# First block of a two-block model: value units first, decay chain inside the attention heads, and a new order at the latent attention's entrance

## The chip, the cores and the metric

One core of a Trainium2 chip (trn2). The metric is the device time of one execution in microseconds (us); smaller is better. Everything runs in one launch.

## The reference

The first block is a hybrid layer on 512 tokens of width 1024. What the change touches:

```python
h = rms_norm(x, mix_norm)
z = h @ w_in                       # 19 column tiles of 128
gq, gk, gv, gr, glr, sq, sk, sv = split_cols(z, SPLITS)
log_a = log_sigmoid(glr @ w_alpha2 + b_alpha) / 16
o_gla = gla_chunked(gq * 64 ** -0.5, gk, gv, log_a)   # 4 heads, chunks of 64
o_gla = rms_norm(o_gla, gla_norm) * silu(gr)
o_swa = swa_sink_attention(rms_norm(sq, q_norm), rms_norm(sk, k_norm), sv, sinks)
                                   # 8 heads, window 128, ALiBi
x = x + concat([o_gla, o_swa]) @ w_out
...                                # convolved, gated feed-forward
```

In `gla_chunked`, b is the running sum of log_a in a chunk; q exp(b) meets k exp(-b) under a causal mask, k exp(b_last - b) makes a state for each chunk, and the states are carried on with the factor exp(b_last). The second block (two layers) has a latent attention, of which the change touches the entrance:

```python
c_kv = rms_norm_2(hn @ w_dkv, kv_norm_g)      # rank 256
k_rope = apply_rope(hn @ w_kr, cos, sin)
k_nope, v = c_kv @ w_uk, c_kv @ w_uv          # 8 heads of 128
q = rms_norm_2(hn @ w_dq, q_norm_g) @ w_uq    # rank 384, 8 heads of 128 + 64
s = (q_nope k_nope^T + q_rope k_rope^T) * 192 ** -0.5, masked, softmax, @ v
```

## The kernel before

**Data.** Activations lie transposed (features on the 128 partitions, 512 tokens along the row), eight tiles for width 1024. Every weight matrix is cut into units of 128 x 1024 numbers, 283 in all (512 KB each), which SyncE loads in order into a ring of four buffers `w_raw`. Float32 accuracy comes from three passes: ScalarE copies a unit to `w_hi` (fp32r), VectorE writes the rest to `w_lo`, and likewise `a_hi`, `a_lo` for activations; `three` multiplies hi by hi, hi by lo and lo by hi. A unit is 24 matmuls of 512 columns. Plain float32 matmuls are used for scores, transposes, sums and spreads.

**Order.** Each engine runs one program written out by hand, and only semaphores tie them together: `unit_ready` (TensorE waits for w_lo), `unit_done` (VectorE waits for the last matmul of a unit), `out_read` (a bank of PSUM has been read), `k_ready` (an operand's low part is there). `w_hi_of(n)` on ScalarE and `lo_ahead(n)` on VectorE prepare the unit three ahead; each waits until its ring slot is free. Waits stand in the queue, so that everything behind one of them waits too.

**The input product** ("z", 19 units): 4 tiles of sliding-window queries (z_sq), keys, values, 4 tiles of linear-attention q and k, the low-rank gate, 4 gate tiles (z_r), and last four units for the linear attention's values, which are computed with tokens on the partitions (`z_v`). At the start `three_tiles` interleaves three tiles over k as the rows of x land, while ScalarE squares each row and GpSimd adds the squares up (`add_squares`); `stat` sums over the partitions, a root and a reciprocal follow, and `spread` brings the factor to all partitions (`r_pre`). Then come tiles 3 and 4, the sums of squares of the five head tiles in a row (`token_sums`), tile 5, the key factors and the turned values.

**The eight window heads** are a pipeline over i from -1 to 7. In a step TensorE makes the scores of head i + 1 (L1244), one z tile, the values of head i - 1 (L1273) and the transposes of head i (L1259). VectorE prepares a w_lo, adds the bias and takes the maximum of head i + 1, normalises head i (L1794), reads the z tile (L1812) and evacuates the transposes. ScalarE prepares a w_hi (L613), takes the exps of head i + 1 (L700) and evacuates the other half (L719).

**The linear attention.** The gate's logits come in steps 4 and 5. Behind the heads, beside the value units, runs the decay chain on two engines: Abs, Exp, Ln (ScalarE), log gate (L1824), two scans (L1827), exps and products. Then scores (L1316), transposes, chunk states, masked products, carried states, and for each head sum of squares, root, factor, spread, gate and split, before the output product ("wout", 8 units, four banks), and "upA".

**The latent entrance** (from 1240 us): units dkv (3), dq (3), uk (2), uq (6), uv (2). A unit's tiles are read by VectorE after the whole unit, rotary embedding is done for each pair of heads after the q units, four products with constants (`run_idle`) stand in front of the first scores, and both value units are done before them.

## Time and profile before

| | |
|---|---|
| median of 3 runs | 1814.08 us (1810.33 to 1817.05) |
| the profiled execution | 1813.4 us, its span on the core 1811.6 us |
| TensorE busy | 1771.5 us (98%) |
| VectorE, ScalarE, GpSimd busy | 986.7, 620.4, 194.3 us |
| mean granted clock of TensorE | 0.992 |

Starts and stretches are in us from the first instruction of the span. Busy times count an engine's own instructions; a stretch in which TensorE is busy throughout can still run at the lower clock, which PEclk shows as a share of full speed.

### The profile page before, as it was taken

To read this page: it belongs to the slowest core of one execution; us is meant where nothing else is said; L and a number is where in the kernel's file an instruction comes from. 1 tells how busy PE (TensorE), PEld (TensorE's weight loads), DVE (VectorE), ACT (ScalarE), POOL (GpSimd) and SP (SyncE) were. 2 spreads that over 40 slices of the span, in tenths; PEclk is the share of its full clock that TensorE was granted. 3 is DMA by queue.
4 is the path that set the end of the run, shared out by engine and by line. 5 is a ranking of instruction groups with operands and counts; after the bars stand their busy time and mean duration, and the time that the engine had idled before them with its cause. 6 is when DMAs were issued, how large, how long until landed. Compare 5 with 4: busy or idle time off the path is not lost.

```text
span 1811.6 us, 21991 instructions
## 1 busy us (share of the span) xinstructions
PE 1771.5 (98%) x8104; PEld 1436.8 (79%) x8104; DVE 986.7 (54%) x1322; ACT 620.4 (34%) x909; POOL 194.3 (11%) x175
## 2 busy tenths in 40 slices
PE   6999999999999999999999999999999999999998
PEld 5777888888888888877888888877767788888886
DVE  4666446673565489985642344346675564234432
ACT  4345234442343342244422222234253433112221
POOL 2100021110011200101110011000000111001111
PEclk9999899999999999999999999999999999999999
DMA  5212023333233222312233233221310223223321
GB/s 181 88 47 70 13 92 113 94 106 115 84 102 100 75 93 93 105 59 94 79 96 104 93 93 102 95 82 58 92 37 1 94 82 104 93 93 95 103 82 46
DMA packets 43844, 156.05 MB, mean 86 GB/s; under 512 B 4864, under 2 KB 4992, under 8 KB 43776
## 3 DMA queue, kind: packets, MB, share of 16 engines
q1 hardware_dynamic: 43632, 154.19, 26.8%
q8 instruction: 46, 0.75, 0.2%
q10 hardware_dynamic: 144, 0.92, 0.1%
q14 instruction: 22, 0.18, 0.0%
HBM read 153.00 MB, written 2.10 MB: 86 GB/s over the span
## 4 chain that ended last, share of the span: by engine, by line
PE 94%; DVE 4%; ACT 1%; issue 1%; DMA 0%; SPq 0%; ACTq 0%; DVEq 0%
PE bank L1023 27%; PE bank L1024 27%; PE bank L1025 27%; PE bank L1168 1%; PE bank L1174 1%; PE bank L1169 1%; PE bank L1244 1%; DVE w_lo L1695 1%; PE bank L1064 1%; PE bank L1273 1%; PE bank L1110 1%; PE bank L1628 1%; PE bank L1098 0%; PE bank L1058 0%; PE bank L1259 0%
## 5 line engine op out<-in xcount | busy, mean ns | idle before, releaser
L1695 DVE TENSOR_TENSOR w_lo<-w_raw,w_hi 128x1024 fp32r<-128x1024 f32 x283 | 364.9, 1292 | 314.3 <-ACT w_hi L613 191.5
L1023 PE MATMUL bank<-a_hi,w_hi 128*128 128x512 f32 x1156 | 460.3, 398 | 20.1 <-DVE w_lo L1695 17.4
L1024 PE MATMUL bank<-a_lo,w_hi 128*128 128x512 f32 x1156 | 455.7, 394 | 0.0
L1025 PE MATMUL bank<-a_hi,w_lo 128*128 128x512 f32 x1156 | 453.5, 392 | 0.0
L1023 PEld LDWEIGHTS bank<-a_hi,w_hi 128*128 128x128 f32 x1156 | 218.7, 189 | 74.6 <-issue 15.1
L1023 PE MATMUL bank<-g_hi,w_hi 128*128 128x512 f32 x688 | 270.1, 393 | 0.0
L1024 PE MATMUL bank<-g_lo,w_hi 128*128 128x512 f32 x688 | 270.0, 392 | 0.0
L1025 PE MATMUL bank<-g_hi,w_lo 128*128 128x512 f32 x688 | 267.6, 389 | 0.0
L1025 PEld LDWEIGHTS bank<-a_hi,w_lo 128*128 128x128 f32 x1156 | 218.4, 189 | 49.1
L1024 PEld LDWEIGHTS bank<-a_lo,w_hi 128*128 128x128 f32 x1156 | 218.9, 189 | 46.2 <-issue 1.0
L613 ACT ACTIVATE w_hi<-w_raw 128x1024 fp32r<-128x1024 f32 x167 | 174.4, 1050 | 196.5 <-PE bank L1025 191.3
L623 ACT ACTIVATE w_hi<-w_raw 128x1024 fp32r<-128x1024 f32 x116 | 121.6, 1048 | 130.3 <-PE bank L1025 130.3
L1025 PEld LDWEIGHTS bank<-g_hi,w_lo 128*128 128x128 f32 x688 | 129.1, 188 | 29.2
L1023 PEld LDWEIGHTS bank<-g_hi,w_hi 128*128 128x128 f32 x688 | 129.2, 188 | 29.1
L1024 PEld LDWEIGHTS bank<-g_lo,w_hi 128*128 128x128 f32 x688 | 129.3, 188 | 26.5
L531 POOL TENSOR_TENSOR tmp<-tmp 128x512 f32<-128x512 f32 x64 | 66.6, 1041 | 490.4 <-DVE tmp L2120 490.4
L926 ACT ACTIVATE g_hi<-tmp 128x512 f32 (+1 forms) x64 | 40.4, 632 | 219.8 <-DVE tmp L2120 219.8
L510 POOL TENSOR_TENSOR ssum<-ssum,tmp 128x512 f32<-128x512 f32 x43 | 62.6, 1455 | 477.5 <-ACT tmp L636 476.3
L2124 DVE TENSOR_TENSOR g_lo<-tmp,g_hi 128x512 f32 (+1 forms) x64 | 44.3, 693 | 89.3 <-POOL tmp L531 89.3
L2010 DVE SCALAR_TENSOR_TENSOR cv<-u_pad,cols,cv 128x512 f32<-128x512 f32 x128 | 91.1, 780 | 0.0
L2120 DVE SCALAR_TENSOR_TENSOR tmp<-bank,r_pre 128x512 f32<-128x512 f32 x64 | 44.2, 690 | 81.1 <-PE bank L1025 76.0
L520 POOL TENSOR_TENSOR tmp<-tmp 128x512 f32<-128x512 f32 x22 | 34.6, 1573 | 283.4 <-ACT tmp L814 283.4
(288 smaller groups left out, 1987.4 us busy)
## 6 DMA issues: line engine op xcount, KB each, us to landing
w_raw<-in_stream SPq DMA_DIRECT2D x283, 512.0 KB, 3.5
h<-in_xT SPq DMA_DIRECT2D x8, 256.0 KB, 6.4
out<-h SPq DMA_DIRECT2D x8, 256.0 KB, 2.1
cst_b<-in_consts SPq DMA_DIRECT2D x1, 896.0 KB, 9.8
cst_b<-in_consts ACTq DMA_DIRECT2D x1, 896.0 KB, 4.5
cols<-in_vectors SPq DMA_DIRECT2D x1, 289.0 KB, 2.8
cst<-in_consts SPq DMA_DIRECT2D x1, 257.0 KB, 8.2
w_al<-in_w_alpha SPq DMA_DIRECT2D x1, 128.0 KB, 9.8
```

Source lines behind the costliest of these rows:

```text
L510: pool.tensor_tensor(ssum[:, :], ssum[:, :], sq_buf[(k - 1) % 2], ALU.add).then_inc(sum_added, 1)
L531: pool.tensor_tensor(tmp[2 + j % 2][:, 0:SEQ], tmp[j % 2][:, 0:SEQ], tmp[j % 2][:, 0:SEQ], ALU.mult).then_inc(hid_sq, 1)
L613: act.activation(w_hi[slot][:, :], w_raw[slot][:, :], ACT.Copy).then_inc(whi_ready, 1)
L623: act.activation(w_hi[slot][:, :], w_raw[slot][:, :], ACT.Copy).then_inc(whi_ready, 1)
L926: act.activation(at(g_hi, 4 * i + j), tmp[j % 2][:, 0:SEQ], ACT.Square)\
L1023: pe.matmul(out, w0, x0, start=start, stop=False, skip_group_check=loose)
L1024: pe.matmul(out, w0, x1, start=False, stop=False, skip_group_check=loose)
L1025: return pe.matmul(out, w1, x0, start=False, stop=stop, skip_group_check=loose)
L1695: dve.tensor_tensor(w_lo[slot][:, :], w_raw[slot][:, :], f(w_hi[slot][:, :]), ALU.subtract)\
L2010: dve.scalar_tensor_tensor(T(cv, c), u_pad[:, c * UW + tap:c * UW + tap + SEQ], col("w_dw", c * CONV_W + tap), T(cv, c), ALU.mult, ALU.add)\
L2120: dve.scalar_tensor_tensor(tmp[j % 2][:, 0:SEQ], bank[j][:, :], 0.0, r_pre[:, :], ALU.max, ALU.mult).then_inc(out_read, 1)
L2124: dve.tensor_tensor(at(g_lo, 4 * i + j), tmp[2 + j % 2][:, 0:SEQ], f(at(g_hi, 4 * i + j)), ALU.subtract).then_inc(x_ready, 1)
```

## The change

It reorders the z product and what hangs on it, and has seven parts.

1. The stream of units starts with the four value units (15 to 18), then keys, z_sq 0 and 1, values of the window heads, low-rank gate, z_sq 2 and 3, q and k, gate tiles. The value units run over x rows in the order in which they land, two rows to a unit. TensorE first multiplies zeros four times (512 columns, float32) as soon as GpSimd has cleared `ssum`. The eight columns of `mix_norm` are loaded ahead of x, the other vectors behind it, and ScalarE takes a root of a constant before x is there.
2. Squares of x go to `m` and are folded by VectorE instead of being summed by GpSimd; their sums over partitions come inside the last value unit.
3. The sums of squares of the head tiles come one at a time inside later tiles; their roots too.
4. The heads begin with eight units done. Logits come in steps 0 and 1, two of the sums of squares in step 2, and the decay chain is spread over steps 2 to 7 on both engines. Two gate tiles are in the heads' last steps.
5. The other two gate tiles are cut in two and stand between the linear attention's parts, as do halves of the first two output tiles. Output tiles go round eight banks. Roots and reciprocals are taken for two heads at once, all sums in one bank.
6. upA's first tiles wait only for the banks they write.
7. Latent entrance: uk and uv tiles are signalled one by one, bank rules name the exact read, w_hi of the first q unit goes ahead of r_post's copy, rope is done a unit earlier with its low parts behind, the products with constants are gone, the second value unit stands behind the first scores, and two output units are prepared in heads 1 and 2.

The diff, cut:

```diff
+Z_UNITS = [15, 16, 17, 18, 4, 0, 1, 5, 10, 2, 3, 6, 7, 8, 9, 11, 12, 13, 14]
...
-IN_M = ("ffpre0", "pre1", "ffpre1")
+IN_M = ("mix", "ffpre0", "pre1", "ffpre1")
...
 # SyncE
-            sp.dma_start(cols[:, :], vectors).then_inc(vec_landed, 16)
+            sp.dma_start(cols[:, 0:KD], vectors[:, 0:KD]).then_inc(vec_landed, 16)
...
+            sp.dma_start(cols[:, KD:], vectors[:, KD:]).then_inc(vec_landed, 16)
...
 # GpSimd
+            pool.memset(ssum[:, :], 0.0).then_inc(zeroed, 1)
             pool.memset(z_sk[:, 0:P], 0.0).then_inc(p_zero, 1)
-            add_squares("mix")
...
 # ScalarE
+            act.wait_ge(v_chain, 1)
+            load_sqrt(len(STATS))
...
-                square("mix", k, T(h, k))
-            w_hi_of(AHEAD, AHEAD)
+                square_in_m(k)
+            for n in range(RING, RING + 3):
+                w_hi_of(n, n % RING)
             act.wait_ge(v_chain, 2)
-            take_root("mix", r_pre)
+            take_root("mix", None)
+            w_hi_of(RING + 3, RING - 1)
+            spread_copy("mix", r_pre)
...
             for i in range(-1, SWA_H):
-                n = z0 + 6 + i + 1
+                n = z0 + 8 + i + 1
                 w_hi_of(n + AHEAD, (n + AHEAD) % RING)
...
+                if i == 3:
+                    act.wait_ge(a_chain, 1)
+                    act.activation(gla_e, gla_e, ACT.Exp, scale=-1.0).then_inc(a_chain, 1)
+                if i == 5:
+                    act.wait_ge(gla_cum, 2)
+                    act.activation(gla_e, gla_b, ACT.Exp, scale=1.0 / 16).then_inc(gla_exp, 1)
+                if i == 6:
+                    act.wait_ge(gla_ops, 1)
+                    act.activation(gla_e, gla_b, ACT.Exp, scale=-1.0 / 16).then_inc(gla_exp, 1)
+                if i == 7:
+                    act.wait_ge(gla_cum, 3)
+                    act.activation(gla_b, gla_b, ACT.Exp, scale=1.0 / 16).then_inc(gla_exp, 1)
                 if i + 1 < SWA_H:
                     swa_exp_of(i + 1)
+                if i == 3:
+                    act.wait_ge(a_chain, 2)
+                    act.activation(gla_e, gla_e, ACT.Ln, bias=1.0).then_inc(gla_l, 1)
...
                     act.activation(swa_pt[i % 2][:, SEQ:], bank[6][:, :], ACT.Copy).then_inc(swa_ea, 1)
+                if i == 0:
+                    gla_logit_of(0)
+                if i == 1:
+                    swa_square(3, T(z_sq, 2), 10)
+                    swa_square(4, T(z_sq, 3), 11)
+                    gla_logit_of(1)
+                if i == 2:
+                    swa_root(3, 2)
+                    act.wait_ge(gla_y, 2)
+                    act.activation(gla_e, gla_b, ACT.Abs).then_inc(a_chain, 1)
...
 # TensorE
-            three_tiles("z", a_hi, a_lo, "mix", "mix")
+            pe.wait_ge(zeroed, 1)
+            for _ in range(4):
+                pe.matmul(bank[7][:, :], ssum[:, 0:P], ssum[:, :], start=True, stop=True)
+            for u in range(4):
+                unit_ready(u)
+                for k in (2 * u, 2 * u + 1):
+                    k_ready("mix", k)
+                    for b in range(NB):
+                        last = three(bank[b][:, :], T(a_hi, k)[:, b * P:(b + 1) * P], T(a_lo, k)[:, b * P:(b + 1) * P],
+                                     T(w_hi[u], k % 2), T(w_lo[u], k % 2), k == 0, k == KD - 1)
+                    if k == 6:
+                        folded_stat("mix")
+                last.then_inc(unit_used, 1)
+            spread("mix")
...
+            gla_scores_of(0)
+            gla_scores_of(1)
+            pe.wait_ge(gla_ops, 3)
+            gla_turn(0)
+            swa_values(SWA_H - 1)
+            gla_turn(1)
+            z_tile(17, 6, 0, 4)
+            pe.wait_ge(gla_tr_read, 2)
+            gla_chunks(0)
+            gla_inner(0)
+            gla_inner(1)
+            z_tile(17, 6, 4)
...
+            gla_chunks(1)
+            gla_carried(0)
+            gla_inner(2)
+            gla_inner(3)
+            z_tile(18, 7, 0, 4)
+            gla_carried(1)
+            gla_mean_square(0)
+            gla_mean_square(1)
+            z_tile(18, 7, 4)
+            gla_factors(0)
+            gla_factors(1)
+            gla_mean_square(2)
+            gla_mean_square(3)
+            wout_part(0, True)
+            gla_factors(2)
+            gla_factors(3)
+            wout_part(1, True)
...
 # VectorE, in the heads' loop, after the z tile is read
+                if i == 2:
+                    swa_r_of(3, 2)
+                if i == 4:
+                    gla_log_gate()
+                    gla_cumulate(0)
+                if i == 5:
+                    gla_cumulate(1)
+                    dve.wait_ge(gla_cum, 2)
+                    dve.tensor_copy(b_last[:, :], chunks[:, :, CHUNK - 1]).then_inc(gla_blast, 1)
+                if i == 6:
+                    dve.wait_ge(gla_exp, 1)
+                    dve.scalar_tensor_tensor(z_q[:, :], z_q[:, :], GLA_DK ** -0.5, gla_e, ALU.mult, ALU.mult)\
+                        .then_inc(gla_ops, 1)
+                if i == 7:
+                    dve.wait_ge(gla_exp, 2)
+                    dve.tensor_tensor(chunks, last.broadcast_to([P, 2 * NCH, CHUNK]), chunks, ALU.subtract)\
+                        .then_inc(gla_cum, 1)
+                    dve.tensor_tensor(gla_e, gla_e, z_k[:, :], ALU.mult).then_inc(gla_ops, 1)
...
 # latent entrance: TensorE
-                last.then_inc(unit_used, 1)
+                    last.then_inc(uk_done if j < 3 else unit_used, 1)
...
-            pe.wait_ge(out_read, TILE0["uv"] + 1)
-            run_idle(0, 4)
-            pe.wait_ge(rope_split, 10)
...
+            uv_tiles(0)
+            pe.wait_ge(rope_split, 10)
             for b in range(NB):
                 mla_scores(0, b)
+            uv_tiles(1)
```

## Rows read from the trace of the kernel before

**Rows 1.** Stretches, core 0: their sum, with each engine's busy time.
```profile
sum 1811.60, PE 1771.55 PEld 1436.83 DVE 986.67 ACT 620.41 POOL 194.28; mean PE 161.05 PEld 130.62 DVE 89.70 ACT 56.40 POOL 17.66
```

**Rows 2.** Stretches: length, busy time (instructions) by engine, PEclk, DMA share, GB/s.
```profile
34.00:67.00 33.00, 30.97 (x167) 26.05 (x168) 11.92 (x16) 12.17 (x18) 3.04 (x2) 0.90 0.26 80
67.00:177.00 110.00, 109.98 (x543) 86.39 (x541) 73.83 (x146) 47.82 (x108) 8.94 (x6) 1.00 0.18 58
...
177.00:206.00 29.00, 24.81 (x257) 23.79 (x256) 16.43 (x37) 10.78 (x20) 1.84 (x2) 0.83 0.11 38
...
180.00:190.00 10.00, 8.63 (x131) 8.10 (x132) 7.12 (x18) 3.89 (x7) 0.00 (x0) 1.00 0.18 63
...
1254.00:1282.00 28.00, 23.59 (x113) 19.24 (x113) 15.37 (x23) 9.01 (x14) 1.28 (x1) 0.94 0.28 85
1282.00:1312.00 30.00, 28.39 (x117) 21.67 (x117) 20.26 (x28) 6.94 (x8) 0.00 (x0) 1.00 0.31 90
1312.00:1342.00 30.00, 26.58 (x121) 19.27 (x122) 24.49 (x45) 18.93 (x40) 0.00 (x0) 1.00 0.21 68
```

**Rows 3.** Waits of TensorE to 300 us: total us, times, longest us.
```profile
PE bank L1023 <- DVE w_lo L1695: 14.7, 3, 9.0
PE bank L1316 <- DVE z_v L1848: 2.8, 1, 2.8
...
PE bank L1023 <- DVE h L1894: 0.9, 1, 0.9
```

**Rows 4.** Timeline, TensorE, entrance: start, duration, engine, line, operation.
```profile
20.31 0.63 PE L1025 MATMUL bank<-a_hi,w_lo 128*128 128x512 f32 x1
20.73 0.63 PE L1023 MATMUL bank<-a_hi,w_hi 128*128 128x512 f32 x1
...
33.25 0.39 PE L1024 MATMUL bank<-a_lo,w_hi 128*128 128x512 f32 x1
33.48 0.39 PE L1025 MATMUL bank<-a_hi,w_lo 128*128 128x512 f32 x1
```

**Rows 5.** Timeline, TensorE: sums of squares (L1058) and head 0's scores (L1244).
```profile
54.63 1.86 PE L1058 MATMUL bank<-cst,tmp 128*128 128x2 f32 x8 [1.36 <-ACT tmp L683]
...
65.46 1.99 PE L1244 MATMUL bank<-z_sk,z_sq 64*128 64x256 f32 x8 [0.27 <-DVE z_sk L1760]
```

**Rows 6.** Timeline of one step of the heads, by engine.
```profile
102.14 1.99 PE L1244 MATMUL bank<-z_sk,z_sq 64*128 64x256 f32 x8
...
111.44 0.98 PE L1259 MATMUL bank<-cst,swa_p 128*128 128x128 f32 x7
...
102.74 1.05 ACT L613 ACTIVATE w_hi<-w_raw 128x1024 fp32r<-128x1024 f32 x1
...
103.82 1.23 DVE L1695 TENSOR_TENSOR w_lo<-w_raw,w_hi 128x1024 fp32r<-128x1024 f32 x1 [0.70 <-ACT w_hi L613]
...
109.88 0.69 DVE L1812 TENSOR_TENSOR z_lr<-bank,r_pre 128x512 f32<-128x512 f32 x1
```

**Rows 7.** Groups of ScalarE, 67 to 165 us: busy us, mean ns.
```profile
L700 ACT ACTIVATE swa_p<-swa_p,small 128x256 f32<-128x256 f32 x32 | 15.8, 494 | 0.0
...
L733 ACT ACT_TABLE_LOAD x1 | 1.3, 1283 | 0.0
```

**Rows 8.** Timeline, VectorE: log gate (L1824) and the two scans.
```profile
165.25 1.23 DVE L1824 SCALAR_TENSOR_TENSOR m<-m 128x1024 f32<-128x1024 f32 x1 [3.73 <-ACT m L733]
...
166.51 2.34 DVE L1827 TENSOR_TENSOR_SCAN m<-cst_b,m 128x512 f32<-128x512 f32 x2
```

**Rows 9.** Waits of TensorE, 1254 to 1345 us.
```profile
PE bank L1023 <- DVE w_lo L1695: 2.7, 1, 2.7
PE bank L1023 <- issue: 1.7, 1, 1.7
...
PE bank L1628 <- DVE q_rot L2200: 1.6, 1, 1.6
```

**Rows 10.** Timeline, TensorE: the products with constants.
```profile
1323.13 3.59 PE L1064 MATMUL bank<-cst 128*128 128x512 f32 x8
```

More of the change, by code:

```diff
@@ L477, in _ @@
             sp.dma_start(w_al[:, :], w_alpha).then_inc(cst_landed, 16)
+            z_rounds = len(Z_UNITS) // RING
+            for n in range(RING, RING + RING * z_rounds):
+                load(n, n % RING)
             def four(i):
@@ new lines, in gla_root_of, with gla_out_of @@
+            def gla_root_of(t):
+                c = RC_GLA + 2 * NB * t
+                act.wait_ge(gla_sums, 2 * t + 2)
+                act.activation(rms[:, c:c + 2 * NB], bank[6][:, 2 * NB * t:2 * NB * t + 2 * NB], ACT.Sqrt,
+                               bias=small[:, 60:61]).then_inc(gla_rms, 1)
+            def gla_out_of(hd):
+                act.wait_ge(o_done, hd + 1)
+                act.activation(T(og_hi, hd), tmp[hd][:, 0:SEQ], ACT.Copy).then_inc(xhi_ready, 1)
+            gla_square(0)
@@ L768, in _ @@
+            gla_square(1)
+            load_sqrt(len(STATS) + 1)
+            gla_root_of(0)
+            gla_square(2)
+            gla_square(3)
+            gla_root_of(1)
+            w_hi_of(UNIT0["wout"] + AHEAD, (UNIT0["wout"] + AHEAD) % RING)
+            silu_of(3)
+            for hd in range(GLA_H):
+                gla_out_of(hd)
             for k in range(8):
@@ new lines, in _, with z_tile, swa_sums_of @@
+            spread("mix")
+            def z_tile(n, bk, first=0, last_k=8):
+                if first == 0:
+                    unit_ready(n)
+                for k in range(first, last_k):
+                    last = three(bank[bk][:, :], T(w_hi[n % RING], k, P), T(w_lo[n % RING], k, P),
+                                 T(a_hi, k), T(a_lo, k), k == 0, k == 7)
+                if last_k == 8:
+                    last.then_inc(unit_used, 1)
+            halves = cst[:, HALVES:HALVES + 2]
+            def swa_sums_of(n):
+                pe.wait_ge(swa_sq, n + 1)
+                if n == 0:
+                    pe.wait_ge(r_ready, 1)
+                token_sums(bank[4][:, 8 * n:8 * n + 8], swa_sq_buf(n), halves).then_inc(swa_sums, 1)
@@ L1225, in _, with sv_transposes @@
                                      cst[:, IDENT:IDENT + P], start=True, stop=True)
             last.then_inc(sk_spread, 1)
-            pe.wait_ge(out_read, 6)
-            for b in range(NB):
-                last = pe.transpose(T(bank[6], b, P), z_lr[:, b * P:(b + 1) * P], cst[:, IDENT:IDENT + P])
-            last.then_inc(sv_turned, 1)
+            z_tile(7, 0, 4)
+            def sv_transposes():
+                pe.wait_ge(out_read, 8)
+                for b in range(NB):
+                    last = pe.transpose(T(bank[6], b, P), z_lr[:, b * P:(b + 1) * P], cst[:, IDENT:IDENT + P])
+                last.then_inc(sv_turned, 1)
@@ L1292, in _, with gla_scores_of @@
                     swa_transpose(i)
[L1294 to L1312 removed]
+            def gla_scores_of(t):
                 for b in range(NB):
@@ L1337, in _, with gla_inner @@
                     last.then_inc(gla_cs, 1)
-            for hd in range(GLA_H):
+            def gla_inner(hd):
                 pe.wait_ge(gla_masked, hd + 1)
@@ L1367, in _, with gla_mean_square, gla_factors @@
                             last.then_inc(gla_o, 1)
-                if t:
-                    gla_mean_square(0)
-                    gla_mean_square(1)
+            def gla_mean_square(hd):
+                pe.wait_ge(gla_sq, hd + 1)
+                if hd == 2:
+                    pe.wait_ge(gla_rms, 1)
+                token_sums(bank[6][:, NB * hd:NB * hd + NB], gla_sq_buf(hd)).then_inc(gla_sums, 1)
+            def gla_factors(hd):
+                pe.wait_ge(gla_r, hd // 2 + 1)
+                if hd >= 2:
+                    pe.wait_ge(gla_gated, hd - 1)
+                for b in range(NB):
+                    last = pe.matmul(T(bank[4 + hd % 2], b, P), r_cols(RC_GLA + NB * hd + b), cst[:, IDENT:IDENT + P],
+                                     start=True, stop=True)
+                last.then_inc(gla_spread, 1)
@@ new lines, in wout_part @@
+            def wout_part(j, first):
+                n = UNIT0["wout"] + j
+                if first:
+                    unit_ready(n)
+                    if j:
+                        pe.wait_ge(o_done, min(j, GLA_H))
+                    else:
+                        pe.wait_ge(out_read, 19)
+                for k in range(0 if first else 4, 4 if first else 8):
+                    k_ready("attn", k)
+                    last = three(wout_bank(j)[:, :], T(w_hi[n % RING], k, P), T(w_lo[n % RING], k, P), *o_tiles(k),
+                                 k == 0, k == KD - 1)
+                if not first:
+                    last.then_inc(unit_used, 1)
@@ L1375, in _ @@
             gla_factors(2)
             gla_factors(3)
-            pe.wait_ge(o_done, GLA_H - 1)
-            tiles("wout", 8, o_tiles, None, "attn")
+            wout_part(1, True)
+            for j in range(8):
+                if j >= 2:
+                    wout_part(j, True)
+                wout_part(j, False)
             def up(name, split, pairs, two_banks=False):
@@ L1599, in _, with uv_tiles @@
                 last.then_inc(unit_used, 1)
-            for u in range(2):
+            def uv_tiles(u):
                 n = UNIT0["uv"] + u
```

509 lines of the change are left out of this document (269 added, 240 removed).

## The prediction

> **What bounds the kernel now.** I read the stretches first. Their sum [rows 1] has TensorE at work for 1771.55 of 1811.60 us, so only its idle time, its time on the low clock and its idle-filling products can be won; making another engine faster pays nothing by itself. The single stretches [rows 2] show where this time lies: idle is the stretch minus the PE column, and the share missing in PEclk, times the stretch, is what the low clock costs. That gives 34 to 67 us: 2.0 idle and 3.3 clock; 177 to 206 us: 4.2 and 4.9; 1254 to 1282 us: 4.4 and 1.7; 1282 to 1312 us: 1.6; 1312 to 1342 us: 3.4, plus the 3.6 us of products with constants [rows 10] that the change removes. From 67 to 177 us the heads leave 0.02 us idle: there nothing can be won, only lost. The lists of waits [rows 3, 9] name what is late; timelines and groups [rows 4 to 8, 10] give durations.
>
> **Entrance.** Now three tiles are interleaved over k, so the first 9 matmuls need three weight units; TensorE waits 14.7 us in three pieces for w_lo [rows 3] and runs at 1.2 GHz until about 22 us (20.31 to 20.73 = 0.42 us per matmul; 33.25 to 33.48 = 0.23 at 2.4 GHz) [rows 4]. The 72nd matmul is over at 33.71. 72 x 0.2285 (0.23, taken finer over a unit) = 16.5, so 17.2 us are lost. Afterwards unit 0 with two rows of x is enough for 24 matmuls (5.5 us), and ScalarE, VectorE and the queue have less than that to do for such a pair (one w_hi of 1.05 and one w_lo of 1.23 [rows 6] beside two operands of half the width and two squares), so the first matmul alone sets the pace. The first x rows no longer queue behind the whole vectors, and Sqrt's table is loaded before they land: I take 8.0 us instead of the 9.0 of the longest wait [rows 3]. Bounds: 7.0 (the load of 1.28 [rows 7] and the transfer both come off) and 9.0 (neither). The four products on zeros start at about 1.3 us; such a product takes 0.9 us at full clock (3.59 for four [rows 10]) and twice that at the low one, so two slow and two fast ones end near 6.7, where TensorE has no work anyway. Won: 17.2 - 8.0 = **9.2**. If they don't warm the clock, some 9 matmuls take 0.42, 1.8 us less won. SyncE's other issues (the split vectors, cst) come behind the x rows and are needed at 28 us; the folds that replace GpSimd's sums (some 3.6 us of VectorE by w_lo's 1.23 for half the first one's width) end near 19 us and are needed then too.
>
> **Sums inside tiles.** The stretch 34 to 67 us loses 5.3 us: 40 little matmuls in a row, a wait of 1.36 us in them [rows 5], and the low clock behind. Afterwards each group lies between parts of a tile, whose 3 us cover reading, squaring and root. Five more switches between kinds of matmul cost 0.15 each. Won: 5.3 - 0.7 = **4.6**. Added up, scores of head 0 start near 60 us, with eight units done instead of six (now 65.46 [rows 5]).
>
> **Decay chain within the heads.** Now it hides behind the value units. The normal head starts at s = 102.14 (scores); values end at s + 9.30, transposes at s + 10.2 [rows 6]. The transposes wait for VectorE, which runs w_lo, softmax input and normalising, 103.82 to 109.88 = 6.06 us, so w_lo must begin by s + 3.2; it begins at s + 1.7, behind w_hi on ScalarE. Spare: 1.5 us. The change puts work ahead of that w_hi in ScalarE's queue, or ahead of the w_lo in VectorE's, and everything beyond the spare is a wait of TensorE, since each head's scores, tile and values take 9.3 us whatever the others do. Head 2: two squares and the second logit are copied behind the previous transposes, the tile waits 0.5. Head 3: behind swa_ea come Sqrt's table (1.28 [rows 7]), the root (0.3), Abs (1.05, w_hi's size): w_lo begins at s + 4.2, wait 4.2 + 6.1 - 9.2 = 1.1. Head 4: Ln's table and Ln (2.3) follow four exps (each 0.49 [rows 7]; 2.3 with sinks) and stand ahead of swa_ea: w_lo at s + 3.6, wait 0.4. Head 5: none, though VectorE has the log gate (1.23) and a scan (1.17) [rows 8] more. Head 6: in the step before, ScalarE waits for both scans, which VectorE makes only when it has read that step's z tile; then come the decay's exp (1.05), the exps of head 6 (2.3) and swa_ea (0.5), and only then the w_hi, which ends at s + 5.7: wait 5.7 + 6.1 - 9.3 = 2.5. Head 7 has no scores to hide behind, values wait 0.7 for the evacuation behind the two exps, transposes 1.4. Then the linear attention's scores wait 2.15 for two VectorE operations of 1.2 each by the log gate's size [rows 8] (subtract, times k). Sum: 0.5 + 1.1 + 0.4 + 2.5 + 0.7 + 1.4 + 2.15 = **8.75 lost**. Bounds: 0 (as in 67 to 177 us) and 16 (if ScalarE's pieces come 1.5 us later still in five places: the spare may be less than the one step shows).
> ACT_TABLE_LOAD is 1283 ns in each row here [rows 7]; the heads get three more. The Trainium skill speaks against this (ScalarE: Activation LUTs, Table sets: the hidden batching unit: group calls by set), and prices a load at about 2.7 us there; by that, heads 3 and 4 would wait 2.8 us more and the kernel take 1792. The trace's own duration decides here.
>
> **Gate tiles within the linear attention.** 177 to 206 us loses 9.1 us [rows 2]: TensorE waits 2.8 for z_v [rows 3] and 1.4 more, then sums, roots and factors follow in turn on the low clock. Afterwards z_v was read 140 us earlier, and parts of two gate tiles and two output tiles (2.85 us each) stand behind each hand-over; the longest of these, the seven chunk states on VectorE, some 2 us, fits in one. og_lo of the last head comes at the k that needs it, within 0.3 us. Six switches cost 0.1 each. Won: **8.5**. Bounds 5 and 9. Up tiles need no longer wait for the last residual: **0.9** [rows 3].
>
> **Latent entrance.** The w_lo wait of 2.7 [rows 9] is not one: k_up's first tile needs bank 0 free, whose read stands on VectorE behind a w_lo that waits for r_post's copy on ScalarE. Now w_hi goes ahead of the copy and the bank rule names the right read; the idle and 1.7 us clock behind go, 4.3 in sum. The wait of 1.7 ("issue") [rows 9] is for 4 reads of k_up after its unit's end; tiles are signalled singly now: 1.7 gone. The products of 3.6 [rows 10] and the 1.6 behind them [rows 9] go, as scores 0 start when rope's lows are ready, and the second value unit (5.5 us) covers the softmax of head 0. One new wait appears: the third tile of the first value unit needs the bank of q tile 10, whose read VectorE makes only after tile 9's unit, one w_lo, one rotation and two lows; TensorE then waits 1.2 us. The three stretches lose 4.4 + 1.7 + 1.6 + 3.4 + 3.6 = 14.7 now [rows 2, 10]; 1.8 stays (that wait and 0.6 in head 0), so 12.9 go. Two weight units prepared in heads 1 and 2 instead of before cost VectorE a w_lo each (1.23 [rows 6]) inside the chain of maxima and lows; I take half of it, 1.2 in sum. Won: 12.9 - 1.2 = **11.7**. Bounds 7 and 13.5.
>
> **Clock.** With 4.3 us of waits and small products in 12 us around the end of the heads I expect one fall to 1.2 GHz; the one in 1254 to 1282 us cost 1.7 us, the one around 54.6 [rows 5] 3.3 [rows 2]. I take **2.0 lost**; bounds 0 and 10 (six falls).
>
> **Sum.** 9.2 + 4.6 - 8.75 + 8.5 + 0.9 + 11.7 - 2.0 = 24.15 us. The profiled execution took 1813.4 (span 1811.60 and 1.8 around it), 0.7 below the median of 1814.08. 1814.1 - 24.2 = **1789.9, say 1789.5**.
>
> **Rivals.**
> - Heads stay covered (queues slack where I have them in series): the 8.75 and the 2.0 are not paid, 1779. For: 0.02 us idle in 110 us now. Against: head 6's chain is an order of waits, not a load. Chance 0.15.
> - Heads cost twice, or the clock falls behind each of their waits (1.6 us for each, six times): 1798 to 1800. For: the low stretches of rows 2 all follow short waits and small matmuls. Against: the 2.8 us wait that ended at 180 us was followed by ten us at full clock [rows 2]. Chance 0.22. The Trainium skill (TensorE: Matmul & The Clock Gate, HAM oscillation) has idle gaps set the clock back to 1.2 GHz each time; the stretch 1254 to 1282 agrees, that from 180 to 190 does not [rows 2].
> - Slower: ScalarE and VectorE wait for each other in every head, so that softmax, decay and weights run in series. From w_lo at s + 7.7 in each of six heads (4 us more each) the 24 us are gone; with 5 us more it is 1819. For: both order the same work by waits, in a fixed queue. Against: VectorE is busy 73.83 of 110 us there [rows 2], 7.4 us per 10.2. Chance 0.04.
> - The change doesn't do what it says: a queue holds back the early starts (entrance and latent part give half): 1800 to 1808. Against: each released wait has a named releaser. Chance 0.09.
>
> **How the numbers follow.** The forecast, 0.5, has its own range 1783 to 1796. The 80% range runs from the covered heads to the doubled ones: 1777 to 1802. A measurement here tells 0.5% (9 us) from nothing: the three runs lie 6.7 us apart. Below 1805: 0.9; 1805 to 1823: 0.06; above: 0.04.
>
> **What would show it.** First weight matmul near 8 us with starts 0.23 apart; head 0's scores near 60; TensorE waits in heads 3 and 6 released by swa_p, 1 and 2.5 us; output tiles done 11 to 14 us earlier than now; no products with constants behind the q tiles, and 1254 to 1342 us shorter by 12 to 13. Wrong it would be made by waits in the heads beyond 12 us in sum, or a PEclk below 0.9 there.

## The result, and the profile after

The changed kernel takes 1791.27 us (median of four, 1787.01 to 1795.35), the kernel before beside it 1814.26 (1810.33 to 1817.05): a ratio of 0.9873, 95% interval 0.9847 to 0.9899. Timed again later (run 9) it took 1787.09 (five times, 1784.24 to 1794.48), ratio 0.9852 (0.9832 to 0.9873). It was forecast at 1789.5, with 1777 to 1802 as the range.

The profiled execution took 1789.78 us, span 1787.6. Its stretches (length, busy time of the engines, PEclk, DMA share, GB/s) answer to [rows 2]:

```profile
34.00:59.00 25.00, 25.00 (x134) 20.90 (x133) 9.43 (x15) 5.82 (x10) 2.99 (x2) 1.00 0.26 85
59.00:156.00 97.00, 90.02 (x460) 70.67 (x458) 67.08 (x142) 47.68 (x110) 10.79 (x8) 1.00 0.15 50
156.00:176.00 20.00, 19.93 (x207) 17.32 (x208) 12.60 (x25) 9.65 (x14) 0.00 (x0) 1.00 0.10 27
176.00:190.00 14.00, 14.00 (x100) 12.27 (x99) 3.87 (x7) 1.73 (x5) 0.00 (x0) 0.88 0.11 39
...
1238.00:1266.00 28.00, 28.00 (x142) 23.44 (x142) 20.18 (x29) 11.02 (x17) 1.29 (x1) 1.00 0.34 109
1266.00:1296.00 30.00, 28.63 (x120) 21.71 (x120) 25.19 (x37) 12.69 (x17) 0.00 (x0) 1.00 0.22 71
1296.00:1326.00 30.00, 28.18 (x154) 22.29 (x153) 22.41 (x50) 17.49 (x46) 0.00 (x0) 1.00 0.17 52
```

The low clock and the idle time ahead of the heads are gone. The heads (59 to 156 us), which left nothing idle before, leave 7.0 us idle. The linear attention (156 to 190) leaves less than 0.1 us idle and has one fall of the clock (0.12 x 14 = 1.7 us). The stretch 1238 to 1266 answers to 1254 to 1282 of before and is full.

TensorE's timeline at the entrance, at the end of the heads and at the sums in the linear attention (start, duration, engine, line, operation, in brackets the idle time before and what ended it):

```profile
1.33 5.11 PE L1279 MATMUL bank<-ssum 128*128 128x512 f32 x8 [1.33 <-POOL ssum L553]
...
8.17 0.50 PE L1098 MATMUL bank<-w_hi,a_hi 128*128 128x512 f32 x1 [1.73 <-DVE w_lo L1851]
...
59.27 1.99 PE L1350 MATMUL bank<-z_sk,z_sq 64*128 64x256 f32 x8
...
90.02 0.47 PE L1098 MATMUL bank<-a_hi,w_hi 128*128 128x512 f32 x1 [0.42 <-issue]
...
110.42 0.98 PE L1365 MATMUL bank<-cst,swa_p 128*128 128x128 f32 x7 [0.97 <-DVE swa_p L1976]
...
143.49 0.98 PE L1365 MATMUL bank<-cst,swa_p 128*128 128x128 f32 x7 [1.84 <-DVE swa_p L1976]
...
150.25 1.74 PE L1379 MATMUL bank<-swa_pt,z_vs 128*64 128x128 f32 x14 [0.26 <-DVE swa_pt L2036]
153.21 0.98 PE L1365 MATMUL bank<-cst,swa_p 128*128 128x128 f32 x7 [1.22 <-DVE swa_p L1976]
...
156.07 1.16 PE L1416 MATMUL bank<-z_q,m 64*128 64x128 f32 x16 [1.88 <-DVE m L2029]
...
179.61 1.05 PE L1136 MATMUL bank<-cst,ssum 128*128 128x1 f32 x8
...
182.17 0.63 PE L1100 MATMUL bank<-a_hi,w_lo 128*128 128x512 f32 x1
```

The first weight matmul starts at 8 us at 2.4 GHz (starts 0.23 apart); head 0's scores follow at 59.27, with eight units done, against 65.46 with six [rows 5]. The waits forecast for the heads stand where they were put; in what follows, head i is the one whose transposes come in the step, beside the scores of head i + 1. The matmul of 0.63 at 182.17 is at 1.2 GHz, right behind sixteen products of one column. The first up tile starts at 235.3 us, before at 251.2: the first block gave 15.9 us. Its last output tile ends 14.9 us earlier, where the prediction's signs had 11 to 14.

Waits of TensorE in the latent part, 1225 to 1400 us (total us, times, longest), and the second of the waits for pt_lo in the timeline:

```profile
PE bank L1098 <- DVE pt_lo L2464: 5.0, 5, 1.6
PE bank L1098 <- DVE q_nope L2417: 1.4, 1, 1.4
PE bank L1798 <- DVE prob_odd L2448: 0.9, 1, 0.9
```

```profile
1315.20 1.25 PE L1798 MATMUL bank<-cst,prob_odd 128*128 128x128 f32 x10
...
1316.56 1.05 ACT L632 ACTIVATE w_hi<-w_raw 128x1024 fp32r<-128x1024 f32 x1
...
1317.51 1.35 ACT L1081 ACTIVATE pt_hi<-bank 128x512 fp32r<-128x512 f32 x3
1318.13 1.62 DVE L2464 TENSOR_TENSOR pt_lo<-bank,pt_hi 128x512 fp32r<-128x512 f32 x3 [2.17 <-ACT pt_hi L1081]
...
1318.96 0.47 PE L1098 MATMUL bank<-pt_hi,v_hi 128*128 128x512 f32 x1 [1.07 <-DVE pt_lo L2464]
```

The waits of [rows 9] and the products of [rows 10] are gone. The wait for q_nope is the one forecast at 1.2. New in size are the waits for pt_lo: a weight's high half stands in ScalarE's queue right ahead of pt_hi, VectorE waits 2.17 us for that, and TensorE 1.07. Up to the scores of head 1 this part gained 13.2 us (they came 1334.0 - 251.2 = 1082.8 us behind the first up tile before, 1304.9 - 235.3 = 1069.6 now), and the whole part only 8.1 in this execution (24.0 us less span, 15.9 of it in the block).

### The profile page after: what moved, and what is told of

Read it like the earlier page. It is cut to its first block, busy times and chain, and to the rows that moved or that the text cites. A ratio compares the mean times of both kernels' runs of the same rounds, so it can differ in the third digit from the quotient of the medians.

```text
span 1787.6 us, 21945 instructions
## 1 busy us (share of the span) xinstructions
PE 1763.8 (99%) x8104; PEld 1431.0 (80%) x8104; DVE 983.1 (55%) x1324; ACT 624.5 (35%) x914; POOL 184.6 (10%) x170
## 4 chain that ended last, share of the span: by engine, by line
PE 92%; DVE 4%; ACT 2%; issue 1%; DMA 0%; SPq 0%; DVEq 0%; ACTq 0%
PE bank L1098 27%; PE bank L1099 27%; PE bank L1100 27%; PE bank L1249 1%; PE bank L1255 1%; PE bank L1250 1%; PE bank L1188 1%; PE bank L1142 1%; DVE w_lo L1851 1%; PE bank L1780 1%; ACT w_hi L632 0%; PE bank L1176 0%; PE bank L1350 0%; PE bank L1136 0%; DVE pt_lo L2464 0%
## 5 line engine op out<-in xcount | busy, mean ns | idle before, releaser
L527 POOL TENSOR_TENSOR ssum<-ssum,tmp 128x512 f32<-128x512 f32 x37 | 52.4, 1417 | 486.7 <-ACT tmp L655 486.2
```

The source lines that it names most:

```text
L527: pool.tensor_tensor(ssum[:, :], ssum[:, :], sq_buf[(k - 1) % 2], ALU.add).then_inc(sum_added, 1)
```

## The experiments

Single times can't tell a move of 1 or 2 us, since executions of one kernel differ by up to 11; for such moves the rows of TensorE decide, which repeat to 0.1 us where no fall of the clock and no stretch of slower matmuls (last section) lies between. The kernel before, timed beside each group on the same chip, took 1815.71 us (runs 1 to 4), 1814.58 (5 to 8) and 1814.74 (9 to 11); runs 1, 2 and 8 to 11 were timed in five rounds, the others have one time and a profile.

**Run 1: the first block alone.** All edits of the latent part (units uk, uq, uv, the heads behind, their queues on ScalarE and VectorE) as before; the rest as changed.

> First block as changed, latent part as in the kernel before. My reading of the trace after: the first block gave 15.9 us and the latent part only 8.1, so this kernel takes about 1798.5. By the prediction's terms (12.45 for the block, 11.7 for the latent part) it would take 1802. A third possibility is that the two are coupled (the clock level or the queues at the entry of the latent part depend on what came 1000 us earlier): then the latent part of this kernel doesn't look as in the kernel before. By the first two, the three stretches from the first value tile of the latent part to head 1 repeat the kernel before, shifted by 15.9 us.

1800.69 us (six, 1794.35 to 1804.06), ratio 0.9922 (0.9904 to 0.9941): 15.0 won, and 11 to 17 by the interval, which holds the prediction's 12.45 as well as the 15.9 of the rows: the timing alone can't tell them apart. Its latent part has the waits of before, 2.7 for w_lo, 1.7 for "issue", 1.6 three times, so the queues of the two parts aren't coupled. The clock did not repeat: PEclk is 1.00 in 1235 to 1265 us, where the kernel before lost 1.7 us in the same code [rows 2] (run 5, which has the first block of before, lost it too). Whether that fall hangs on the first block or is the execution's is open.

**Run 2: the latent part alone.** The complement.

> First block as in the kernel before, latent part as changed. Reading of the trace: about 1806 (8.1 won); by the prediction's term 1802.5 (11.7 won). The heads of the latent part should show the same waits for the low half of the transposed probabilities as the changed kernel (0.7, 1.1, 1.6, 0.7). Whether the clock falls after the last head, 1.6 us in the changed kernel and nothing in the one before behind the same two waits, is open: if it falls here too, it belongs to the change; if not, it is chance.

1805.14 us (five, 1802.51 to 1805.49), ratio 0.9943 (0.9927 to 0.9959): 10.6 won. The waits for pt_lo are there, five and 5.0 us. The fall of the clock behind the last head is not: in 1352 to 1425 us PEclk is 1.00. The parts give 15.0 + 10.6 = 25.6, both together 23.0 and 27.7 in the two timings. The interval of this run, 7 to 13 us, holds the 8.1 of the profiled execution as well as the 11.7 of the prediction. What the profiled execution lost behind the last head (1.8 us of low clock and a slower output product, below) is not in this one's rows.

**Run 3 and run 10: the decay's exponentials behind those of the heads.**

```diff
-                if i == 5:
-                    act.wait_ge(gla_cum, 2)
-                    act.activation(gla_e, gla_b, ACT.Exp, scale=1.0 / 16).then_inc(gla_exp, 1)
-                if i == 6:
-                    act.wait_ge(gla_ops, 1)
-                    act.activation(gla_e, gla_b, ACT.Exp, scale=-1.0 / 16).then_inc(gla_exp, 1)
...
                 if i + 1 < SWA_H:
                     swa_exp_of(i + 1)
+                if i == 5:
+                    act.wait_ge(gla_cum, 2)
+                    act.activation(gla_e, gla_b, ACT.Exp, scale=1.0 / 16).then_inc(gla_exp, 1)
+                if i == 6:
+                    act.wait_ge(gla_ops, 1)
+                    act.activation(gla_e, gla_b, ACT.Exp, scale=-1.0 / 16).then_inc(gla_exp, 1)
```

> In the changed kernel, the two exponentials of the decay that stand ahead of the softmax exponentials of heads 6 and 7 in ScalarE's queue are put behind them. The prediction's mechanism (an order of waits: softmax of head 6 is held until VectorE has made both scans): TensorE's wait of 1.8 us in head 6 goes to under 0.3, that of 1.2 in head 7 shrinks to about the 0.7 that VectorE's own work costs; the linear attention's scores start about 2.3 us earlier (156.1 to 153.8). Rival, VectorE's load is the cause (log gate, scans and product are 4.9 us more in these steps): the waits stay as they are, and the scores of the linear attention start within 0.5 us of 156.1.

1778.3 us. Waits of TensorE from 59 to 160 us:

```profile
PE bank L1365 <- DVE swa_p L1976: 1.4, 2, 1.0
PE bank L1416 <- DVE m L2029: 1.1, 1, 1.1
...
```

The waits of heads 6 and 7 are gone altogether (head 7's 0.26 and 1.22 too, of which I had left 0.7), and the scores of the linear attention wait 1.1 in place of 1.9. From head 0's scores to those it is 92.5 us against 96.8: 4.3 us, where I had expected 2.3. VectorE does the same work as before in these steps, so its load was not the cause; the order of waits in ScalarE's queue was. It shows there, in the changed kernel and then in run 3:

```profile
132.77 1.06 ACT L754 ACTIVATE m<-m 128x1024 f32<-128x1024 f32 x1 [8.94 <-DVE m L1988]
133.74 0.28 ACT L727 ACTIVATE small<-small,cols 128x4 f32<-128x4 f32 x1
...
136.37 1.05 ACT L632 ACTIVATE w_hi<-w_raw 128x1024 fp32r<-128x1024 f32 x1
```

```profile
129.11 0.30 ACT L727 ACTIVATE small<-small,cols 128x4 f32<-128x4 f32 x1 [5.75 <-DVE small L1965]
...
132.30 1.06 ACT L763 ACTIVATE m<-m 128x1024 f32<-128x1024 f32 x1 [0.93 <-DVE m L1988]
...
133.74 1.05 ACT L632 ACTIVATE w_hi<-w_raw 128x1024 fp32r<-128x1024 f32 x1
```

ScalarE stood idle for 8.94 us behind a wait for the scans while the softmax's work lay queued behind it. In run 3 that work is over when the scans come. The second timing, run 10:

> Run 3 once more, timed. Its one time of 1778.3 was 13 below the changed kernel's median, while its rows show 4.2 us of waits less and one fall of the clock (1.7) less in the first block; the convolution's stage, untouched, showed no low clock there (3.4 us in the changed kernel's profile). Theory: 5.9 belong to the move, the rest is the execution: median near 1785.5. Rival, all of it is the move's: 1778 to 1780.

1780.50 us (five, 1779.33 to 1781.48), ratio 0.9812 (0.9798 to 0.9825), 6.6 below the changed kernel beside it (run 9), by the two intervals 2 to 11. So 13 is out, but my median of 1785.5 was missed by 5 us, and 1780.50 lies close to the rival's 1778 to 1780. I had reckoned it from 1791.3, and the changed kernel itself took 1787.09 here. The rows of the two profiled executions, 7.1 us apart in their spans, have 4.3 in the heads, as in run 3, and 3.0 between the linear attention's scores and the latent heads, which this edit doesn't touch (run 9 has low clock in the convolution's stage, PEclk 0.96, and slower matmuls in 196 to 252 us); run 10's first weight came 0.3 later. Of the 5.9, the 1.7 for a fall of the clock isn't in them: run 9 has none behind the heads either. What is shown for the move is 4.3 us.

**Run 4: two output units behind the last latent head.**

```diff
-                if i in (1, 2):
-                    w_hi_of(UNIT0["wo"] + i + 1, (UNIT0["wo"] + i + 1) % RING)
...
+            for i in (1, 2):
+                w_hi_of(UNIT0["wo"] + i + 1, (UNIT0["wo"] + i + 1) % RING)
             after("wo", "post1", 1, 1)
```

VectorE's `lo_ahead(UNIT0["uv"] + i)` moves likewise.

> In the changed kernel, the two weight units of the output product that are prepared in latent heads 1 and 2 are prepared behind the last head instead. Theory: these two pairs of copies are what lengthens the steps of heads 0 to 3 from 7.25 us to 7.9, 8.2, 8.7 and 7.8; without them TensorE's waits there fall from 4.1 us in sum to about 1, and the last head ends 3 us earlier against its first scores; the output product behind has 5.6 us per tile and hides both copies. The prediction's term would have this at 1.2 us. Rival: what lengthens the heads is the second value unit's low parts and weight copy ahead of them on VectorE, a backlog that is worked off head by head: then less than 1 us is won.

1784.82 us. Waits, 1225 to 1400 us:

```profile
PE bank L1098 <- DVE pt_lo L2464: 1.7, 2, 0.9
PE bank L1098 <- DVE w_lo L1851: 1.5, 1, 1.5
...
```

From head to head (starts of the scores of heads 1 to 6) the changed kernel needs 7.9, 8.2, 8.7, 7.8 and 7.3 us, this one 7.9, 7.3, 7.2, 7.3 and 7.3: 2.9 us are the two units'. The prediction had 1.2; the backlog theory falls. The steps tell the engines apart. The second holds only a w_hi (0.9 us longer), the third a w_hi and a w_lo (1.5), the fourth only a w_lo (0.5): some 0.9 for each w_hi on ScalarE and 0.5 for each w_lo on VectorE. Without the w_hi, pt_hi starts 1.36 us behind the transposes of head 1, where it was 2.31 (1317.51 - 1315.20):

```profile
1314.01 1.25 PE L1798 MATMUL bank<-cst,prob_odd 128*128 128x128 f32 x10
...
1315.37 1.35 ACT L1079 ACTIVATE pt_hi<-bank 128x512 fp32r<-128x512 f32 x3
```

What I had wrong in the expectation is "hides both": the first three output tiles run together and need the third unit at once, 1.5 us of new wait. The output product takes 1.8 us longer (47.5 against 45.7), so of the 2.9 only 1.1 are kept by this move.

**Run 5: the spare time of a step.** In the kernel before, useless copies ahead of w_hi in the steps that have the scores of heads 2, 4 and 6:

```diff
+                for j in {1: (0,), 3: (1, 2), 5: (3, 4, 5)}.get(i, ()):
+                    if j:
+                        act.wait_ge(junk_done, j)
+                    act.activation(gla_e, h[:, 0:1024], ACT.Copy).then_inc(junk_done, 1)
                 w_hi_of(n + AHEAD, (n + AHEAD) % RING)
```

> In the kernel before, copies of 1.05 us that nobody needs are put ahead of the weight's high half in ScalarE's queue: one in the step of head 2's scores, two in that of head 4's, three in that of head 6's. The prediction's model of a step (1.5 us of spare, all beyond it is a wait of TensorE): nothing, 2.1 - 1.5 = 0.6 and 3.15 - 1.5 = 1.65 us of waits at the transposes, 2.3 in sum, and steps of 9.3 us in between. Rival of covered heads (the queues have slack): nothing at all three. Rival of coupled queues: each step is late by the whole of the added work, and the next one too: 6.3 us or more.

1816.46 us. The timeline of TensorE has these waits in the heads and no other:

```profile
112.38 0.98 PE L1265 MATMUL bank<-cst,swa_p 128*128 128x128 f32 x7 [0.47 <-DVE swa_p L1800]
135.79 0.98 PE L1265 MATMUL bank<-cst,swa_p 128*128 128x128 f32 x7 [1.20 <-DVE swa_p L1800]
```

Nothing for 1.05 us, 0.47 for 2.1, 1.20 for 3.15 (forecast 0, 0.6, 1.65). The spare is 1.6 us in the second (2.1 - 0.47) where I read 1.5. It is 2.0 in the third (3.15 - 1.20), a step that is longer by the gate's logit product, as the same step of the kernel before is (11.07 us for 10.2). Nothing passes on to the next step. Of the three models only the prediction's gives this.

**Run 6: no products on zeros.** The wait for `zeroed` and the four products are left out.

> The changed kernel without the four products on zeros ahead of the first weight. Prediction: the first nine or so matmuls run at 1.2 GHz, 0.42 us each in place of 0.23, and all behind starts 1.8 us later (head 0's scores at 60.6 in place of 58.8). Rival, operands set the pace anyway: the scores of head 0 start within 0.4 us of 58.8. The time itself can't tell this from the spread of executions; the rows can.

1787.69 us. The entrance:

```profile
7.89 0.80 PE L1098 MATMUL bank<-w_hi,a_hi 128*128 128x512 f32 x1 [7.89 <-DVE w_lo L1848]
8.49 0.63 PE L1099 MATMUL bank<-w_lo,a_hi 128*128 128x512 f32 x1
...
11.89 0.39 PE L1098 MATMUL bank<-w_hi,a_hi 128*128 128x512 f32 x1
```

Nine matmuls at 1.2 GHz, 0.43 apart, until 11.9 us, and head 0's scores at 60.79. The first weight itself comes at 7.7 to 8.2 us by execution; from its first matmul to head 0's scores it is 52.9 us here and 51.1 in each of the nine profiles with the products and the new first block. The 1.8 holds.

**Run 7: the low half of the second value unit later.**

```diff
-                if 2 <= u < 5:
+                if 2 <= u < 4:
                     lo_ahead(n)
+                if u == 5:
+                    lo_ahead(n - 1)
```

> In the changed kernel, VectorE makes the low half of the second value unit behind its reads of q tiles 10 and 11 in place of ahead of them. The prediction's mechanism for the third tile of the first value unit (its bank's read stands behind a w_lo, a rotation and two lows): the wait of 1.4 us goes to about 0.1, and the scores of head 0 start 1.3 us earlier. Rival, the rotation and its lows alone hold it: the wait shrinks by less than 0.3. A second rival: the 1.2 us come back as a wait at the first scores, since rope's last lows are then the late ones: the scores don't move.

1793.6 us. Waits, 1225 to 1400 us:

```profile
PE bank L1780 <- DVE a_hi L2432: 1.0, 1, 1.0
...
PE bank L1098 <- DVE q_nope L2417: 0.2, 1, 0.2
```

1.4 went to 0.2, so the mechanism was right, and 1.0 came back at the first scores, which wait for the low parts of the first value unit that VectorE makes behind the moved w_lo; the move is worth 0.2 us. The place was the second rival's, the late operation another than it said.

**Run 8: the three moves together.**

> The changed kernel with the three moves together: the two exponentials behind those of the heads, the two output units behind the last latent head, the low half of the second value unit behind q tiles 10 and 11. By the stretches of the runs so far: 4.2 us of waits and 1.7 of low clock in the first block, 2.9 in the latent heads, 1.3 ahead of them, 10.1 in all, so 1781 us at the median against 1791.3, a ratio to the kernel before of 0.981. If the single run of the exponentials alone, at 1778.3, were all due to that move, 1774. If the falls of the clock are chance and come with any order, 1783.

1783.76 us (five, 1778.37 to 1785.74), ratio 0.982 (0.9794 to 0.9846). That is nearest to the 1783 of the expectation. The rows have the gains in the heads (92.5 us from scores to scores; 56.6 from latent head 1's scores to the output product, against 59.5 to 61.1 with the units in the heads), but not all of the 10.1: the third output unit takes 1.8 back (run 4) and the first scores 1.0 (run 7). The profiled execution is longer, too, by its matmuls in 260 to 620 us, the next point.

**Run 9: the changed kernel again.**

> The changed kernel itself once more, for the spread and beside the two below. Runs 7 and 8 had matmuls at 233.3 ns in place of 228.9 from 14 us into the first up-projection to its loop's end 360 us later, at a granted clock of 1.00, which costs 6.8 us. Theory: that is drawn anew in each execution, so the times of this kernel spread over some 8 us (1787 to 1795 so far) and its profile may show either. Rival: it belongs to the order at the start of that stage in runs 7 and 8: then this profile shows 228.9 and all times lie within 5 us.

1787.09 us (1787.55, 1787.09, 1794.48, 1784.24, 1785.18); its profile (1787.55) shows 228.9 ns per matmul throughout that stage, as the rival had it. The spread of 10 is more than the rival allows. So neither came out whole, and the last section takes it up.

**Run 11: five moves.** As run 8, but the third output unit in the last head, the second value unit's low half behind `v_lo_of(0)`, and Abs at the head of the next step:

```diff
                 if i + 1 < MLA_H:
                     mla_exp_of(i + 1, 3)
+                else:
+                    w_hi_of(UNIT0["wo"] + 2, (UNIT0["wo"] + 2) % RING)
...
             v_lo_of(0)
+            lo_ahead(UNIT0["uq"] + 4)
             lo_ahead(UNIT0["uq"] + 5)
...
                 if i == 3:
+                    act.wait_ge(gla_y, 2)
+                    act.activation(gla_e, gla_b, ACT.Abs).then_inc(a_chain, 1)
                     act.wait_ge(a_chain, 1)
```

> As run 8, with its losses mended: the third output unit is prepared in the last latent head behind ScalarE's and VectorE's copies of the transposed probabilities, where both stand idle for 2 us (the first three output tiles run together, and run 8 waited 1.5 us for this unit); the low half of the second value unit behind the low parts of the first (run 8 waited 1.0 us for those); and the log gate's absolute value at the head of the next step (the wait of 1.0 in head 3). Expected: these three waits under 0.2 each, 3.3 us less than run 8 by the rows, so a median near 1780 and a ratio to the kernel before of 0.981. Rival: the absolute value moved makes head 4's wait (0.45) grow by what head 3 loses.

1776.19 us (1775.03, 1775.90, 1776.19, 1782.15, 1782.32), ratio 0.9795 (0.9780 to 0.9810): the fastest here, 10.9 below the changed kernel beside it. Its waits, 59 to 160 us and then 1225 to 1400:

```profile
PE bank L1417 <- DVE m L2030: 1.1, 1, 1.1
PE bank L1366 <- DVE swa_p L1977: 0.7, 2, 0.4
```

```profile
PE bank L1099 <- DVE pt_lo L2466: 1.9, 2, 1.0
...
```

Head 3's wait went from 0.97 to 0.23, not quite the 0.2 expected, and head 4's stayed at 0.45; the other two are gone, and the output product takes 45.7 us again. The five times fall into two groups 6 us apart, and the profiled one is of the slower.

## Why the prediction was right, point by point

The total was 24.15; the two timings give 23.0 and 27.7. Part of that closeness is luck: in the profiled executions the first block gave 15.9 us where its terms add up to 12.45, and the latent part 8.1 where 11.7 stood, and the two misses cancel. The terms of the prediction, and what the rows say:

| term | forecast | measured | how |
|---|---|---|---|
| entrance and sums inside tiles | 9.2 + 4.6 = 13.8 | 14.6 | 65.46 - 59.27, two units more (11.0) done by then, two groups of sums (1.9) and four transposes (0.7) not yet |
| waits in the heads | -8.75 | -7.0 | 97.0 - 90.0 busy, 59 to 156 us |
| linear attention, up tiles | 8.5 + 0.9 = 9.4 | 10.0 | the rest of the block's 15.9, not measured alone |
| clock | -2.0 | -1.7 | 0.12 x 14 us; one or two falls, by execution |
| latent part to head 1 | 12.9 | 13.2 | scores of head 1, from the first up tile; 1.7 of it a low clock before, not there in run 1 |
| two output units in the latent heads | -1.2 | -2.9 | run 4, the heads alone |
| sum | 24.15 | 26.2 | |

The profiled executions differ by 24.0 us; the 2.2 missing from 26.2 are for the most part the fall of the clock behind the last latent head (1.8) and the slower output product behind it (0.9), told below, which run 2 and run 9 don't show.

**Entrance.** 8.0 us for the first weight was right (8.17 for the first on the timeline, 7.89 in run 6), and so was 1.8 us for the products on zeros. The other terms up to head 0's scores, and the 10.0 of the linear attention, are differences of rows; no run takes their moves apart.

**Heads.** The model of a step, a fixed order with 1.5 us of spare, was the right one; run 5 measured the spare alone. Head by head: 0.42 of 0.5, 0.97 of 1.1, 0.45 of 0.4, none of none, 1.84 of 2.5, 0.26 of 0.7, 1.22 of 1.4, 1.88 of 2.15. Six of the seven waits came out shorter than forecast. The spare explains little of that: in heads 3, 4 and 6 the wait is the start of w_lo less s + 3.25 to s + 3.33, and the prediction had s + 3.2. Head 6's is short because its w_hi ended at s + 5.14 (137.42 us, s = 132.28) and not at s + 5.7. ScalarE's rows of head 3 are those of the working: Sqrt's table, the root, Abs, and w_lo at s + 4.2 (s = 100.08).

```profile
100.81 1.28 ACT L710 ACT_TABLE_LOAD   x1
102.10 0.27 ACT L710 ACTIVATE rms<-bank,small 128x16 f32<-128x16 f32 x1
102.27 1.05 ACT L787 ACTIVATE m<-m 128x1024 f32<-128x1024 f32 x1
103.22 1.05 ACT L632 ACTIVATE w_hi<-w_raw 128x1024 fp32r<-128x1024 f32 x1
```

All five table loads in the heads took 1283 ns. One stood there before, so four were new and not the three that the prediction counts; the two that load Exp's table again (104.29 and 115.02 us) are followed by 2.3 and 3.4 us in which ScalarE is idle, and no wait comes of them. The Trainium skill (ScalarE: Activation LUTs, Table sets) prices a load at about 2.7 us. The measurement disagrees, for the whole switch too: the copy ahead of the load above ends at 100.79 us and the root starts at 102.10.

**Latent part.** The step of the prediction that was mis-sized is "Two weight units prepared in heads 1 and 2 ... cost VectorE a w_lo each (1.23 [rows 6]) inside the chain of maxima and lows; I take half of it, 1.2 in sum": run 4 measured 2.9. VectorE's w_lo, which I priced at 0.6 each, cost 0.5. What I put at nothing is the w_hi, which stands ahead of pt_hi on ScalarE in a chain (transposes, pt_hi, pt_lo, values) that TensorE waits for: it takes 1.05 us and 0.9 of that was paid each time.

**Rivals.** Covered heads (1779) are out by 7 us of waits; with one order changed 2.9 of them are left (run 3) and the median is 1780.50 (run 10). Doubled heads are out by their sum; that the clock falls behind the waits is half true, next section. My own term had one fall around the end of the heads: in the changed kernel's profile there was none there and one behind the sums of the linear attention, so in that execution its size was right and its place was not. Coupled queues are out by run 5, and a change that does only half by the first weight at 8.17 us and the 13.2 us of the latent entrance.

## What to carry to other kernels

Where an engine's queue is a fixed order, price an inserted operation by what it takes beyond the spare time of its step, and on every engine that has a part in it; a wait inserted into a queue costs what is queued behind it, so put it behind all that doesn't need it (here 4.3 us of waits for two exponentials). A unit prepared "in the heads" costs least where both engines stand idle, as in the last head, and a move out of the heads has to be counted where the unit is needed too (run 4 won 2.9 us and paid back 1.8). Terms that add up to the right total can hide misses that cancel: compare them one by one. Where the change is a sum of moves of 1 to 5 us, read them from rows that repeat to 0.1 us, and not from single times.

## What the runs showed of the hardware

**Two rates of a matmul at one granted clock.** Runs 7, 8 and 11 show, at PEclk 1.00 and in untouched code, starts 233.3 ns apart from 30 us behind the first up tile on, for 360 us, where the ten other profiles show 228.9. Over 360 us that is 6.8 us. Run 11 and then run 9, the same stage:

```profile
300.16 0.40 PE L1100 MATMUL bank<-a_lo,w_hi 128*128 128x512 f32 x1
300.39 0.40 PE L1101 MATMUL bank<-a_hi,w_lo 128*128 128x512 f32 x1
300.63 0.40 PE L1099 MATMUL bank<-a_hi,w_hi 128*128 128x512 f32 x1
```

```profile
300.20 0.39 PE L1100 MATMUL bank<-a_hi,w_lo 128*128 128x512 f32 x1
300.43 0.39 PE L1098 MATMUL bank<-a_hi,w_hi 128*128 128x512 f32 x1
300.65 0.39 PE L1099 MATMUL bank<-a_lo,w_hi 128*128 128x512 f32 x1
```

Two readings stand. A rate drawn anew in each execution fits run 11's two groups of times, 6 us apart at one mean clock (0.999), and run 9's 1794.48, 7 us above two others of the same mean clock (0.997). But the three profiles are just the three whose kernels have the low half of the second value unit moved on VectorE (about a microsecond's work, 1000 us later), and none of the ten others shows it; a draw without any tie to the kernel would pick just these three of the thirteen once in 286 times. Only one execution of each timing was profiled, so neither reading is shown, and the cause is open. Shorter stretches at 233.3 are in every profile (around 660 to 700 us, for one), and some come and go in the same code: the changed kernel's first profile has it over the output product behind the latent heads (1366 to 1410 us), 0.9 us, and run 9's in 196 to 252 us, 0.7 us, but not there.

**The clock falls by execution too.** Behind the heads it fell in 155 to 160 us in run 1 (PEclk 0.71) and not in the changed kernel's own profile of the same code. Over the six executions with the heads' waits it fell right behind them in four (runs 1, 4, 6, 7) and behind the sums of the linear attention in five; over the four with the exponentials moved (runs 3, 8, 10, 11) in none and in three. Each fall costs 1.6: from the linear attention's scores to the first up tile it is 77.6 us with none (run 3), 79.2 with one (79.9 in run 9, with its slower matmuls), 80.7 with two. So the waits of 1 to 2 us at the end of the heads seem to bring falls, but not each and not always; four executions against six is little to go by. The Trainium skill (TensorE: Matmul & The Clock Gate, HAM oscillation) has an idle gap set the clock back each time; the waits of heads 2 to 6, 0.4 to 1.9 us, brought none in any run. Its own example has longer gaps than these, so they don't test it there. Behind the last latent head the same two waits of 0.9 were followed by the low clock in the changed kernel (first row, PEclk 0.84, 1.8 us) and by the full one in the kernel before (second row):

```profile
1357.00:1368.00 11.00, 9.09 (x44) 0.84 0.01 1
```

```profile
1383.00:1394.00 11.00, 9.07 (x51) 1.00 0.01 1
```

And the convolution's stage, which no kernel here changes, lost 3.4 us to the clock in some executions (PEclk 0.96 over 84 us in the kernel before) and none in others (run 10, 1.00 over 85 us). Falls of the clock and slower matmuls like these are of the size of the spread, 5 to 11 us, among the times of one kernel; that they make all of it isn't shown, with one profile for each timing.
